# Two layers of a diffusion backbone on one core: the bias of the layer norms added by GpSimd

## What is computed

```python
def layer_norm(x, g, b):
    mu = jnp.mean(xf, axis=-1, keepdims=True)
    var = jnp.mean(jnp.square(xf - mu), axis=-1, keepdims=True)
    y = (xf - mu) * lax.rsqrt(var + EPS) * g + b
...
    y = jnp.concatenate([att, m_out, g_out], axis=-1) @ w_out
    x = layer_norm(DEEPNORM_ALPHA * x + g1 * y, ln1_g, ln1_b)
    h2 = x * (1 + sc2) + sh2
    f = jnp.square(jax.nn.relu(h2 @ w_ff1)) @ w_ff2
    x = layer_norm(DEEPNORM_ALPHA * x + g2 * f, ln2_g, ln2_b)
```

## Time and profile before

| | |
|---|---|
| median of three runs | 3866.44 us (3858.68 to 3870.52) |
| the profiled execution's own time | 3864.26 us |
| its span | 3862.4 us |
| TensorE busy | 3279.2 us (85%) |
| VectorE busy | 1700.5 us (44%) |
| ScalarE busy | 910.0 us (24%) |
| GpSimd busy | 492.6 us (13%), 519 instructions |
| mean granted TensorE clock | 0.897 of 2.4 GHz |

### The profile page before, as it was taken

One profiled execution on the slowest core, in us unless ns is written; L12 is line 12 of the kernel. 1 busy time (PEld: TensorE's weight loads), 2 busy tenths in 40 slices (PEclk: granted clock), 3 DMA queues, 4 the chain that ended last, 5 costly groups with the idle time before them and its releaser, 6 DMA issues.

```text
span 3862.4 us, 43139 instructions
## 1 busy us (share of the span) xinstructions
PE 3279.2 (85%) x16208; PEld 2617.6 (68%) x16208; DVE 1700.5 (44%) x3038; ACT 910.0 (24%) x1686; POOL 492.6 (13%) x519
## 2 busy tenths in 40 slices
PE   5996665998879999999949966659988799999995
PEld 4775443555668888889838854435557799999994
DVE  3114565553743333333481145655536433333337
ACT  2112212442221121112222222124422222222221
POOL 2000122010420000000150001220104200000004
PEclk8997556999989999999979976569989899999998
DMA  4431000001122222221311110000011111111113
GB/s 183 136 122 34 0 8 8 0 0 71 71 70 75 76 81 83 84 70 41 115 71 44 44 34 0 8 9 0 0 71 71 44 44 44 44 44 44 40 37 120
DMA packets 95221, 207.05 MB, mean 54 GB/s; under 512 B 12496, under 2 KB 13072, under 8 KB 94544
## 3 DMA queue, kind: packets, MB, share of 16 engines
q1 hardware_dynamic: 78240, 151.76, 12.3%
q0 software_dynamic: 16816, 53.02, 3.7%
HBM read 185.29 MB, written 19.44 MB: 53 GB/s over the span
## 4 chain that ended last, share of the span: by engine, by line
PE 71%; DVE 11%; issue 8%; POOL 4%; DVEq 2%; DMA 2%; POOLq 1%; ACT 1%; ACTq 0%; SPq 0%
PE ps L1408 17%; PE ps L1411 17%; PE ps L1412 17%; PE ps L1610 6%; PE ps L1586 3%; DVE nm L1220 2%; PE ps L1597 2%; PE ps L1390 2%; DVE hf L881 1%; PE ps L1598 1%; PE ps L1500 1%; PE ps L1534 1%; POOL acc L476 1%; POOL xr L476 1%; POOLq L472 1%
## 5 line engine op out<-in xcount | busy, mean ns | idle before, releaser
L1408 PE MATMUL ps<-hi,w_hi 128*128 128x384 f32 x1584 | 538.7, 340 | 58.4 <-POOLq L345 40.0
L1412 PE MATMUL ps<-hi,w_lo 128*128 128x384 f32 x1584 | 532.6, 336 | 0.0
L1411 PE MATMUL ps<-lo,w_hi 128*128 128x384 f32 x1584 | 532.2, 336 | 0.0
L1408 PE MATMUL ps<-w_hi,f_hi 128*128 128x512 f32 x1152 | 460.2, 400 | 33.4 <-DVE acc L1312 33.4
L1411 PE MATMUL ps<-w_lo,f_hi 128*128 128x512 f32 x1152 | 453.4, 394 | 0.0
L1412 PE MATMUL ps<-w_hi,f_lo 128*128 128x512 f32 x1152 | 452.5, 393 | 0.0
L401 DVE TENSOR_TENSOR w_lo<-w_raw,w_hi 128x512 fp32r<-128x512 f32 x368 | 258.9, 740 | 389.3 <-ACT w_hi L396 388.9
L396 ACT CAST w_hi<-w_raw 128x512 fp32r<-128x512 f32 x368 | 215.2, 619 | 868.6 <-PE ps L1408 807.0
L1408 PE MATMUL ps<-w_hi,hi 128*128 128x512 f32 (+1 forms) x1008 | 383.7, 381 | 17.8 <-DVE xr L1273 10.3
L1312 DVE TENSOR_TENSOR acc<-acc,ps 128x512 f32<-128x512 f32 x288 | 196.1, 686 | 419.7 <-PE ps L1412 419.5
L1411 PE MATMUL ps<-w_lo,hi 128*128 128x512 f32 (+1 forms) x1008 | 379.5, 377 | 0.0
(11 more groups left out here) (252 smaller groups left out, 4157.1 us busy)
## 6 DMA issues: line engine op xcount, KB each, us to landing
w_raw<-in_w_slots SPq DMA_DIRECT2D x368, 256.0 KB, 3.0
w_raw<-in_m_slots SPq DMA_DIRECT2D x160, 256.0 KB, 2.8
x_dram<-xr POOLq DMA_DIRECT2D x18, 512.0 KB, 3.0
x1t<-x_dram POOLq DMA_DIRECT2D x6, 1536.0 KB, 14.7
out<-acc POOLq DMA_DIRECT2D x18, 512.0 KB, 3.0
modw<-in_w_mod SPq DMA_DIRECT2D x4, 2048.0 KB, 9.0
acc<-in_x_in SPq DMA_DIRECT2D x3, 1536.0 KB, 15.8
xr<-in_x_in POOLq DMA_DIRECT2D x1, 4608.0 KB, 15.3
```

Source lines behind the costliest of these rows:

```text
L1408: mm = pe.matmul(out, a_hi, b_hi, start=first, stop=False)
L1411: pe.matmul(out, a_hi, b_lo, start=False, stop=False)
L1412: return pe.matmul(out, a_lo, b_hi, start=False, stop=last)
```

## The change

The addition of the bias goes from VectorE to GpSimd, for both norms of both layers, 36 tiles of 128x1024. GpSimd multiplies the tile by the gain, drains, adds the bias and itself signals `xr_done` or `y_rdy`. The semaphore `ln_g` and VectorE's function `offset` are gone. The store of a tile is issued at the same place of GpSimd's loop as before; what it waits for is now signalled by its own engine, one turn earlier.

```diff
-            def norm_rows(L, w, x, gain, store):
+            def norm_rows(L, w, x, gain, bias, done, store):
...
                     if 1 <= t <= NT:
                         pool.wait_ge(S["ln_x"], NT * (2 * L + w) + t)
-                        pool.tensor_tensor(x[:, t - 1], x[:, t - 1], gain, ALU.mult).then_inc(S["ln_g"], 1)
+                        pool.tensor_tensor(x[:, t - 1], x[:, t - 1], gain, ALU.mult)
+                        pool.drain()
+                        pool.tensor_tensor(x[:, t - 1], x[:, t - 1], bias, ALU.add).then_inc(done, 1)
                     if t > 1:
                         store(t - 2)
...
-                norm_rows(L, 0, xr, lnb[:, 0], store1)
+                norm_rows(L, 0, xr, lnb[:, 0], lnb[:, 1], S["xr_done"], store1)
...
-                norm_rows(L, 1, acc, lnb2[:, 0], store2)
+                norm_rows(L, 1, acc, lnb2[:, 0], lnb2[:, 1], S["y_rdy"], store2)
...
-            def offset(L, w, x, t, bias, done):
-
-                dve.wait_ge(S["ln_g"], NT * (2 * L + w) + t + 1)
-                dve.tensor_tensor(x[:, t], x[:, t], bias, ALU.add).then_inc(done, 1)
...
                     if t < NT:
                         residual(1, t)
                         statistics(xr, t)
-                    if t > 1:
-                        offset(L, 0, xr, t - 2, lnb[:, 1], S["xr_done"])
...
                         statistics(acc, t)
-                    if t > 1:
-                        offset(L, 1, acc, t - 2, lnb2[:, 1], S["y_rdy"])
```

More of the change, by code:

```diff
@@ L327, in build @@
             yT_ps y_hi y_lo o_out xr_half ln_ld xr_done x1_st
-            h_ps r_done fhi_done flo_done f_ps f_acc acc_zero ln_in ln_rs ln_x ln_g y_rdy ln_st""".split()
+            h_ps r_done fhi_done flo_done f_ps f_acc acc_zero ln_in ln_rs ln_x y_rdy ln_st""".split()
         S = dict((n, sem(n)) for n in names)
```

## The result

| | median | runs | ratio to before, 95% interval |
|---|---|---|---|
| before | 3867.09 us | 3858.68 to 3870.52 | |
| changed | 3902.72 us | 3900.84 to 3907.40 | 1.0097 (1.0079 to 1.0116) |

The changed kernel is 0.97% slower, by 35.6 us. The profiled execution took 3900.84 us with a span of 3899.1 us, 36.7 above the span before. The forecast was 3901.

A forecast was written before the change was run, and what follows sets the result against it. It took GpSimd's turn to be on the path in norm 1 and VectorE's turn to set norm 2's pace. 5.8 + 10.2 + 7.6 + 11.4 = +35.0 us on 3864.3, plus 2.2 for the median, gave 3901; range 3884 to 3920.

The forecast's parts named there:

- A: The forecast itself: each engine gets the shared SBUF port when the other drains; 3901 us, chance 0.62.
- B: Rival: GpSimd keeps the port over its drain, so the gate waits longer in norm 2; 3917 us, chance 0.20.
- C: Rival, not slower: in norm 2 VectorE's gate and residual fit beside GpSimd's rsqrt, drain and store; 3875 us, chance 0.06.
- D: Rival: the drain before `nbias` gets short once VectorE's addition is gone from beside the store; about 3890 us, chance 0.08.
- The chain of ports: Norm 2: product, gate, GpSimd's addition and residual run one after another; turn 9.70 us, 1.23 more than 8.47.
- The low parts: Norm 1, layer 0: GpSimd begins them 13.5 us later, plus 1.2 for VectorE's splits falling into its last turns.
- 21.3 + X: Norm 1's second half: chain of low parts, modulated tiles, four splits and high part; 26.0 us, against 34.9 before in layer 0.
- X: Time of four VectorE weight splits in norm 1's second half: 2.48 to 6.88 us, the middle taken.
- GpSimd's turn is on the path: Norm 1: TensorE ends its projection by 1039, then waits for GpSimd's last low part, though GpSimd is 13% busy.
- the phase ends 3.7 later: Norm 2, layer 0: the phase ends 3.7 us after its last store is issued; that norm in all +7.6 us.
- the 0.5: End of norm 2, layer 1: two stores close together may cost 0.5 us more.
- The four terms: Norm 1 +5.8 us in layer 0 and +10.2 in layer 1; norm 2 +7.6 and +11.4; sum +35.0.

The follow-up runs named there:

- store_moved: The changed kernel with GpSimd's store of tile t-2 issued behind `nbias`, ahead of the next product; 3872.42 us, 1.0014 of before.
- n2_only: The changed kernel with GpSimd adding the bias in norm 2 alone, VectorE adding it in norm 1 as before; 3885.82 us, 1.0048 of before.
- apart: The kernel before, in norm 2 GpSimd's product held until VectorE's residual of the next tile, VectorE's addition moved ahead of the gate; 3846.32 us, 0.9953.
- no_bias: The changed kernel with the bias addition left out on both engines; 3833.63 us, 0.9913 of before.
- before_store_moved: The kernel before with GpSimd's store of a tile issued behind `nbias`, ahead of the next product; 3878.59 us, 1.0031 of before.
- apart_store: The kernel apart with the store issued behind `nbias` in both norms; 3846.22 us, 0.9951 of before.
- no_gap: The changed kernel with the addition of the tile before straight behind this tile's product, no drain between; 3930.63 us, 1.0164 of before.

## Why the prediction held

*A against B, C and D.* The chain of ports was right to about 0.1 us: the gate was forecast at 3.1 and took 3.22, the residual 3.3 and took 3.25, the turn 9.70 and was 9.76 (9.71 in the mean of seven). B's gate of 5.5 did not appear. D was excluded twice: the gap before `nbias` stayed with VectorE's additions gone, and in store_moved went with the store. It is 1.96 us (1050.77 to 1052.72) even while VectorE stands idle, from 1043.05 to the split at 1054.73. So it doesn't come from VectorE's hold on the ports; it lasts until the store has landed (see the last section). The rule of the Trainium skill that I cited for D (page "SBUF — State Buffer", section "SBUF: two separate sides") doesn't explain it in this kernel; the page's own case is a VectorE instruction in a two-port mode. C's interleaving exists, but the changed kernel doesn't fall into it, since each turn starts again from `rs`, as I had argued.

*Norm 1.* The low parts were forecast 14.7 us later and came 15.0 later. The second half was put at 21.3 + X with X 4.68; it was 27.4 (1065.40 to 1092.81) with X 6.13 in layer 0 and 6.12 in layer 1. So the term "X, the middle" was 1.45 too small, nearly all of the 1.6 by which norm 1 of layer 0 missed. In layer 1 the same term was off, and the total by 0.8. What I had not seen is that the pattern of before in layer 1 (X of 2.48) was chance: in n2_only and apart, with norm 1 unchanged, it didn't come back (7.11 to 7.41). About 4 us of the difference between the two profiles in layer 1 are that pattern: against n2_only's 95.4 us the changed norm costs 6.6, not 11.0. How often the runs fall into it isn't known.

*Whose turn is on the path.* I wrote that "GpSimd's turn is on the path". For the changed kernel that holds as it stands: from the rsqrt of tile 2 on GpSimd never waits for VectorE's statistics, its low parts start straight behind its last store (1065.38 and 1065.40), and the chain that ended last runs through it up to the first of them. TensorE's 5.44 us a tile keeps rs(0) to rs(8) at 43.5 to 44.8 us in before, changed and no_bias, so GpSimd's turns of 8.05 to 8.70 us show as a backlog that is paid behind rs(8). For the kernel before it holds with a limit that I didn't state: GpSimd's turn of 5.65 is only 0.2 us above TensorE's 5.44, so a shorter one gains almost nothing. My expectations for before_store_moved and apart_store failed on that: in apart_store GpSimd's turn fell to 4.9, and rs(0) to rs(8) only from 44.3 to 43.7. (One reading in the prediction is a tile off: the wait of 2.02 us stands behind the store of tile 0; from the store of tile 1 on there is none.)

*Norm 2.* Layer 1 was right (+11.2 for +11.4). Layer 0 was 2.4 short, in the term "the phase ends 3.7 later". The timeline of GpSimd at the end of norm 2 of layer 0, changed kernel, which answers to the earlier trace rows:

```profile
2003.17 1.19 POOL L611 DMA_DIRECT2D out<-acc  x2
2010.37 0.54 POOL L490 DMA_DIRECT2D rcon<-in_row_in  x1 [6.01 <-POOLq L345]
```

The last of the two stores is issued at 2003.83, 13.2 us after rs(8), with 12.9 forecast; but the phase ended 5.8 us after it, not 3.7. The 3.7 came from layer 1 of before, where a single store goes out alone. The DMA view tells what is different, layer 0 (2000 to 2010 us) and then layer 1 (3890 to 3899); the last number of a row is the median time from issue to landing in us:

```profile
w_raw<-in_w_slots SPq DMA_DIRECT2D x6, 256.0 KB, 4.4
out<-acc POOLq DMA_DIRECT2D x2, 512.0 KB, 4.5
...
out<-acc POOLq DMA_DIRECT2D x2, 512.0 KB, 3.4
```

In layer 0 four loads of weights are issued between 2003.80 and 2005.60, beside the two stores. The last store landed 5.53 us after its issue, at 2009.36, and the phase ended at 2009.67. In layer 1, with no load beside them, the last of the pair landed after 3.73 us and the span ended 4.5 after its issue; the 0.5 that the prediction added for two stores close together had no row behind it, and was 0.8. No run was made without the loads.

*The total.* The four terms came to +39.7 for +35.0, and 3.0 us of ordinary difference elsewhere hid most of that; a part of the hit is luck.

## What to carry to other kernels

On these two engines, the load of each says little about where elementwise work with two SBUF inputs should go: what counts is the sum of both engines' time on the ports in a stage, and GpSimd needs 2.4 us for what VectorE does in 1.2. Look in a timeline for one form that has two durations (1.22 and 3.10): the difference is a collision, and a semaphore that orders the two engines can be worth more than moving work. Before counting a turn as a cost, check which engine feeds the stage; a backlog costs only what is left of it when the feeder ends. For the same reason a shorter turn gains nothing once it is below the feeder's. And a drain placed right behind a store costs what the store still needs to land: in these loops 1.4 to 1.9 us a turn, and nothing where the store stood behind `nbias`.

## What was not expected of the hardware

- A drain of GpSimd that follows a store which it has issued ends only when the store has landed. In about 150 such places in these traces GpSimd's next instruction starts 0.16 to 0.22 us after the landing, also where the landing is late (see the table). A store mostly lands 2.9 to 3.0 us after its issue; with the store 0.64 ahead of rsqrt, rsqrt to `nbias` is therefore 2.5 us, with the store elsewhere 0.7. In no_bias, norm 2, where the store is over 4 us old at the rsqrt, the gap is 0.2.

| | store issued | landed | next instruction behind the drain |
|---|---|---|---|
| changed | 1041.52 | 1044.49 | 1044.67 |
| changed | 1032.82 | 1036.42 | 1036.59 |
| store_moved | 1051.58 | 1055.78 | 1055.95 |
| no_gap | 1072.49 | 1076.71 | 1076.93 |

- A semaphore that GpSimd signals and then itself waits for costs 0.6 us between the two instructions (0.57 to 0.64 in no_gap).
- Who gets the ports next is not settled. VectorE got in between two instructions of GpSimd with a drain (changed) and without one (no_gap), but a request made during the issue of a store, with a product ready behind it, was passed over (3.50 us above), and the first split beside three low parts stood 6.15 us. I found no one rule for these; none of the runs separates them.
